# Chunked RWKV scan on one core: odd chunks cross the partition halves, and crossing and straight 64x64 products alternate

## What is computed

```python
def step(st, inp):
    r_t, w_t, k_t, v_t, a_t, b_t = inp
    sa = jnp.einsum('dbhij,dbhj->dbhi', st, a_t)
    st = st * w_t[..., None, :] + sa[..., None] * b_t[..., None, :] + v_t[..., None] * k_t[..., None, :]
    y = jnp.einsum('dbhij,dbhj->dbhi', st, r_t)
    return st, y
```

## Time and profile before

| | us |
|---|---|
| median of 3 runs | 3831.46 |
| lowest and highest | 3827.92 and 3834.9 |
| the profiled execution's own time | 3832.17 |
| its span in the trace | 3830.4 |
| the scan stage in the trace | 3019.6 to 3382.5 |

### The profile page before, as it was taken

How to read it: one execution, slowest core, us unless ns; L and a number is a source line. 1 busy time by engine, 2 the same in 40 slices (tenths; PEclk the granted TensorE clock), 3 DMA queues, 4 the chain that set the end, 5 groups by cost and what they waited for, 6 DMA issues and landing times.

```text
span 3830.4 us, 74936 instructions
## 1 busy us (share of the span) xinstructions
PE 3743.3 (98%) x30266; PEld 3432.7 (90%) x30266; DVE 2649.1 (69%) x3847; ACT 1868.0 (49%) x2450; POOL 0.2 (0%) x4
## 2 busy tenths in 40 slices
PE   8999999999999999999999999999999999999997
PEld 7999988999898888899988888888889899999896
DVE  6799977887755774667766656565766766666565
ACT  4444445444554544477455545454545433356653
POOL 0000000000000000000000000000000000000000
PEclk9999999999999999999999999999999999999999
DMA  5555544435554556544555555555564311134453
GB/s 194 176 182 185 176 146 163 163 118 195 186 176 171 195 185 220 190 154 169 191 182 187 187 187 189 187 187 190 176 227 156 123 58 47 47 117 154 163 195 134
DMA packets 99110, 634.90 MB, mean 166 GB/s; under 512 B 10864, under 2 KB 14320, under 8 KB 28720
## 3 DMA queue, kind: packets, MB, share of 16 engines
q1 hardware_dynamic: 98832, 631.00, 48.2%
HBM read 622.53 MB, written 8.42 MB: 165 GB/s over the span
## 4 chain that ended last, share of the span: by engine, by line
PE 88%; DVE 7%; ACT 2%; issue 1%; DMA 1%; SPq 0%; DVEq 0%; ACTq 0%
PE ps_gemm L355 33%; PE ps_gemm L344 18%; PE ps_gemm L357 17%; PE ps_gemm L341 6%; DVE ring_r L279 2%; PE ps_gemm L2107 2%; PE ps_aux L2107 2%; DVE arena L1384 1%; ACT w_hi L273 1%; PE ps_gemm L2066 1%; PE ps_aux L2066 1%; DVE arena L1681 1%; PE ps_aux L1794 1%; PE ps_gemm L2055 1%; PE ps_aux L1239 1%
## 5 line engine op out<-in xcount | busy, mean ns | idle before, releaser
L279 DVE TENSOR_TENSOR ring_r<-ring,w_hi 128x1024 fp32r<-128x1024 f32 (+3 forms) x1260 | 1411.7, 1126 | 876.5 <-ACT w_hi L273 862.0
L273 ACT ACTIVATE w_hi<-ring 128x1024 fp32r<-128x1024 f32 (+3 forms) x1260 | 1226.6, 979 | 1249.2 <-PE ps_gemm L355 703.8
L355 PE MATMUL ps_gemm<-arena_r,w_hi 128*128 128x512 f32 x5824 | 1471.4, 395 | 23.6 <-ACT w_hi L273 13.1
L355 PEld LDWEIGHTS ps_gemm<-arena_r,w_hi 128*128 128x128 f32 x5824 | 1052.2, 190 | 217.9 <-issue 23.1
L357 PEld LDWEIGHTS ps_gemm<-arena_r,ring_r 128*128 128x128 f32 x5824 | 795.6, 191 | 70.6 <-DVE ring_r L279 14.1
L357 PE MATMUL ps_gemm<-arena_r,ring_r 128*128 128x256 f32 x5824 | 814.9, 283 | 9.8 <-DVE ring_r L279 9.6
L344 PE MATMUL ps_gemm<-arena_r,w_hi 128*128 128x256 f32 (+2 forms) x4896 | 660.5, 284 | 7.8 <-ACT w_hi L273 6.8
L344 PEld LDWEIGHTS ps_gemm<-arena_r,w_hi 128*128 128x128 f32 (+2 forms) x4896 | 615.7, 190 | 13.3 <-ACT w_hi L273 7.5
L344 PE MATMUL ps_gemm<-arena_r,ring_r 128*128 128x256 f32 (+3 forms) x2448 | 364.7, 285 | 13.3 <-DVE ring_r L279 13.1
L344 PEld LDWEIGHTS ps_gemm<-arena_r,ring_r 128*128 128x128 f32 (+3 forms) x2448 | 321.2, 190 | 21.3 <-DVE ring_r L279 19.7
L1384 DVE SCALAR_TENSOR_TENSOR arena<-arena,vecs (+15 forms) x480 | 192.0, 462 | 0.0
(11 more groups left out here) (363 smaller groups left out, 2541.9 us busy)
## 6 DMA issues: line engine op xcount, KB each, us to landing
ring<-in_ff SPq DMA_DIRECT2D x128, 1024.0 KB, 4.9
ring<-in_w_out SPq DMA_DIRECT2D x48, 1024.0 KB, 4.9
ring<-in_gate SPq DMA_DIRECT2D x32, 1024.0 KB, 4.9
ring<-in_conv_a SPq DMA_DIRECT2D x16, 1024.0 KB, 5.3
ring<-in_conv_b SPq DMA_DIRECT2D x16, 1024.0 KB, 4.9
ring<-in_gla_v SPq DMA_DIRECT2D x16, 1024.0 KB, 4.9
ring<-in_conv_z SPq DMA_DIRECT2D x16, 1024.0 KB, 4.9
ring<-in_conv_out SPq DMA_DIRECT2D x16, 1024.0 KB, 4.9
```

The source lines that it names most:

```text
L273: nc.scalar.activation(w_hi[q % 2][:, 0:size], ring[slot][:, part], ACT.Copy).then_inc(hi_ready, 1)
L279: nc.vector.tensor_tensor(ring_lo[slot][:, part], ring[slot][:, part], w_hi[q % 2][:, 0:size].bitcast(F32), ALU.subtract).then_inc(lo_read ...
L355: mm = nc.tensor.matmul(halves, w, r_both[:, :, kk, :], start=q == 0 and k == 0, stop=False)
```

## The change

For odd chunks the two heads swap partition halves in every matrix that is indexed by token: `crossed` turns the output's half around for c = 1 and 3. Products from channel-indexed to token-indexed data, and back, then read one half of the partitions and write the other ("crossing"); for even chunks, and for all products of token by token, they stay in their half ("straight"). In tok, gram and the first half of w, `paired` issues a straight and a crossing product in turn; the results of even chunks go to one bank of XY and those of odd chunks to the other (`banked` tells the copies where they are). Where one bank (or the y bank) changes between straight and crossing writers, TensorE waits for its own earlier matmul: two new waits for `tiles_turned` per direction and iteration, five for `y_turned` per iteration. `TERMS` has a new order: the 22 terms are now spread as 4, 4, 2, 4, 1, 5, 2 over the seven places, before as 4, 4, 4, 4, 2, 2, 2. The number and shape of the matmuls is the same, on every engine.

```diff
-                q.XY = ps[:, 2:4, :].rearrange("p b n -> p (b n)") if d == 0 else ps[:, 0:2, :].rearrange("p b n -> p (b n)")
+                q.XY = ps[:, 2:4, :] if d == 0 else ps[:, 0:2, :]
...
+            def crossed(R, c):
+                return HALVES[1 - HALVES.index(R)] if c % 2 else R
+            def banked(bank2, blocks, n):
+                return bank2[:, :, 0:blocks * 2 * n].rearrange("p a (g n) -> p g a n", n=n)
+            def paired(straight, cross):
+                for pair in zip(straight, cross):
+                    for emit in pair:
+                        for R in HALVES:
+                            x = emit(R)
+                return x
...
                 if name == "tok":
-                    b = by(q.bk[:, 0, :])
-                    each(q.Z, AR[:, :, 0, :], b)
-                    v = by(channels(VD, it))
-                    for k, src in enumerate((AR[:, :, 0, :], by(q.bkp[:, 0, :]), by(q.bkp[:, 1, :]), v)[0:4 - d]):
-                        for c in range(NCH):
-                            for R in HALVES:
-                                x = mm(q.XY[R, (NCH * k + c) * CH:(NCH * k + c + 1) * CH], src[R, c, :], ident[R, R], start=True, stop=True)
+                    b, v = by(q.bk[:, 0, :]), by(channels(VD, it))
+                    sources = (AR[:, :, 0, :], by(q.bkp[:, 0, :]), by(q.bkp[:, 1, :]), v)[0:4 - d]
+                    def grams(c):
+                        return lambda R: mm(q.Z[crossed(R, c), c * CH:(c + 1) * CH], AR[R, c, 0, :], b[R, c, :], start=True, stop=True)
+                    def turned(k, c):
+                        at = (2 * k + c // 2) * CH
+                        return lambda R: mm(q.XY[crossed(R, c), c % 2, at:at + CH], sources[k][R, c, :], ident[R, R], start=True, stop=True)
+                    by_k = range(len(sources))
+                    paired([grams(0), grams(2)], [turned(0, 1), turned(0, 3)]).then_inc(tiles_turned, 1)
+                    paired([turned(k, c) for k in by_k for c in (0, 2)][:-2], [turned(k, c) for k in by_k[1:] for c in (1, 3)])
+                    pe.wait_ge(tiles_turned, 4 * it + d + 1)
+                    return paired([turned(by_k[-1], 0), turned(by_k[-1], 2)], [grams(1), grams(3)])
                 elif name == "gram":
-                    for k, bank in ((1, q.X), (0, q.Y)):
-                        for c in range(NCH):
-                            for R in HALVES:
-                                x = mm(bank[R, c * P:(c + 1) * P], q.bk[R, k, c * CH:(c + 1) * CH],
-                                       AR[R, c, :, :].rearrange("p k n -> p (k n)"), start=True, stop=True)
+                    def grams(k, c):
+                        at = (2 * k + c // 2) * P
+                        return lambda R: mm(q.XY[crossed(R, c), c % 2, at:at + P], q.bk[R, k, c * CH:(c + 1) * CH],
+                                            AR[R, c, :, :].rearrange("p k n -> p (k n)"), start=True, stop=True)
+                    return paired([grams(k, c) for k in (1, 0) for c in (0, 2)], [grams(k, c) for k in (1, 0) for c in (1, 3)])
...
                 elif name == "w":
-                    each(X0, q.tok[:, 0], q.TT)
-                    x = each(X1, q.TT, q.Z0)
+                    def weights(c):
+                        at = c // 2 * CH
+                        return lambda R: mm(q.XY[crossed(R, c), c % 2, at:at + CH], q.tok[R, 0, c, :], q.TT[R, c, :], start=True, stop=True)
+                    paired([weights(0), weights(2)], [weights(1), weights(3)]).then_inc(tiles_turned, 1)
+                    for c in (0, 2, 1, 3):
+                        if c == 1:
+                            pe.wait_ge(tiles_turned, 4 * it + d + 3)
+                        at = (2 + c // 2) * CH
+                        for R in HALVES:
+                            x = mm(q.XY[R, c % 2, at:at + CH], q.TT[R, c, :], q.Z0[R, c, :], start=True, stop=True)
                 elif name[0] == "u":
                     c = q.order[name[1]]
                     for R in HALVES:
-                        x = mm(q.Y[R, 0:CH], q.W1T[R, c, :], q.S[R, name[1], :], start=True, stop=True)
+                        x = mm(q.Y[crossed(R, c), 0:CH], q.W1T[R, c, :], q.S[R, name[1], :], start=True, stop=True)
                 elif name[0] == "s":
                     c = q.order[name[1]]
                     for R in HALVES:
-                        mm(q.Z[R, 0:CH], q.tok[R, 1, c, :], q.U[R, c, :], start=True, stop=False)
+                        mm(q.Z[crossed(R, c), 0:CH], q.tok[R, 1, c, :], q.U[R, c, :], start=True, stop=False)
                     for R in HALVES:
-                        x = mm(q.Z[R, 0:CH], q.tok[R, 2, c, :], VT[R, c, :], start=False, stop=True)
+                        x = mm(q.Z[crossed(R, c), 0:CH], q.tok[R, 2, c, :], VT[R, c, :], start=False, stop=True)
                 return x
-            TERMS = {("s", 0): (("v", 0), ("v", 1)), ("u", 1): (("v", 2), ("v", 3)), ("s", 1): (("u", 0), ("s", 1)), ("u", 2): (("u", 1), ("s", 2)),
-                     ("s", 2): (("u", 2),), ("u", 3): (("s", 3),), "end": (("u", 3),)}
-
-            def outputs(it, step):
+            TERMS = {("s", 0): (("v", 0, 0), ("v", 0, 1), ("v", 2, 0), ("v", 2, 1)),
+                     ("u", 1): (("v", 1, 0), ("v", 1, 1), ("v", 3, 0), ("v", 3, 1)),
+                     ("s", 1): (("u", 1, 0), ("u", 3, 1)),
+                     ("u", 2): (("u", 0, 0), ("u", 2, 1), ("s", 1, 0), ("s", 2, 1)),
+                     ("s", 2): (("u", 1, 1),),
+                     ("u", 3): (("u", 2, 0), ("s", 2, 0), ("s", 1, 1), ("s", 3, 0), ("s", 0, 1)),
+                     "end": (("u", 0, 1), ("u", 3, 0))}
+            TURNED = {("u", 1): 1, ("u", 2): 2, ("s", 2): 3, ("u", 3): 4}
+            def outputs(pe, it, step):
                 y = dirs[1].X
-                for kind, k in TERMS[step]:
-                    for d, q in enumerate(dirs):
-                        c = k if kind == "v" else q.order[k]
-                        left, right = {"v": (VT[:, c, :], q.M2[:, c, 1, :]), "u": (q.U[:, c, :], q.M1[:, c, 1, :]), "s": (q.S[:, k, :], q.AR[it % 2][:, c, 1, :])}[kind]
-                        for R in HALVES:
-                            x = nc.tensor.matmul(y[R, c * CH:(c + 1) * CH], left[R, :], right[R, :], start=step == ("s", 0) and k == 0 and d == 0,
-                                                 stop=step == "end" and d == 1, skip_group_check=True)
+                if step in TURNED:
+                    pe.wait_ge(y_turned, 5 * it + TURNED[step])
+                for kind, c, d in TERMS[step]:
+                    q = dirs[d]
+                    left, right = {"v": (VT[:, c, :], q.M2[:, c, 1, :]), "u": (q.U[:, c, :], q.M1[:, c, 1, :]),
+                                   "s": (q.S[:, q.order.index(c), :], q.AR[it % 2][:, c, 1, :])}[kind]
+                    if step == "end" and d == 0:
+                        x.then_inc(y_turned, 1)
+                        pe.wait_ge(y_turned, 5 * it + 5)
+                    for R in HALVES:
+                        x = nc.tensor.matmul(y[R if kind == "s" else crossed(R, c), c * CH:(c + 1) * CH], left[R, :], right[R, :],
+                                             start=step == ("s", 0) and c == 0 and d == 0, stop=step == "end" and d == 0, skip_group_check=True)
+                if step in (("s", 0), ("s", 1), ("u", 2), ("s", 2)):
+                    x.then_inc(y_turned, 1)
                 return x
...
-                    return cp(q.tok, q.XY[:, 0:256 * (4 - d)].rearrange("p (k c n) -> p k c n", k=4 - d, c=NCH))
+                    return cp(q.tok.rearrange("p k (g a) n -> p (k g) a n", a=2), banked(q.XY, 4 - d, CH))
...
-                    m = per_chunk(masks64[:, d, :, :].rearrange("p k t -> p (k t)"))
-                    for bank, M in ((q.X, q.M2), (q.Y, q.M1)):
-                        x = tt(M.rearrange("p c k t -> p c (k t)"), by(bank), m, ALU.mult)
+                    m = masks64[:, d, :, :].rearrange("p (a b k) t -> p a b (k t)", a=1, b=1).broadcast_to([P, 2, 2, P])
+                    for k, M in ((1, q.M2), (0, q.M1)):
+                        x = tt(M.rearrange("p (g a) k t -> p g a (k t)", a=2), banked(q.XY[:, :, k * 2 * P:(k + 1) * 2 * P], 1, P), m, ALU.mult)
```

More of the change, by code:

```diff
@@ L2029, in rwkv_scan @@
             VT = dirs[0].tok[:, 3]
-            prep_exp, chain, y_done, y_copied, started = stage_sems("exponentials", "dve_chain", "y_done", "y_copied", "states_zero")
+            prep_exp, chain, y_done, y_copied, started, y_turned, tiles_turned = stage_sems("exponentials", "dve_chain", "y_done", "y_copied", "states_zero", "y_tiles_turned", "tiles_turned")
             prepared = stage_sems("prepared0", "prepared1")
@@ L2097, in rwkv_scan, with pe_emit @@
             HALVES = (slice(0, CH), slice(CH, P))
+            def crossed(R, c):
[8 more added lines that the diff above has]
+                return x
             RATE = float(np.exp(-0.5))
-            def pe_emit(it, q, d, name):
+            def pe_emit(pe, it, q, d, name):
```

(8 more changed lines are left out.)

## The result

The changed kernel takes **3818.95 us** (median of 11 runs, 3815.12 to 3822.12); the kernel before took 3830.41 us in runs on the same chip (11 runs, 3827.0 to 3836.26). The ratio is 0.9969, with a 95% interval of 0.9962 to 0.9977: faster by 0.3%, 11.5 us. The forecast was 3817, 14.4 us from tok and gram. The profiled execution took 3819.21 us at a span of 3817.4.

The account below looks back on a forecast made before the run. TensorE is busy 98% of the span, but VectorE is late next and limits the gain. 3832.2 us less 7 x 2.06 = 14.4, plus 0.3, is 3818.1; the median lies 0.7 lower, say 3817; range 3809 to 3837.

Parts of the forecast that it names:

- tok and gram: Main term, scan stage: paired products let d2 start 2.06 us earlier in seven iterations, 14.4 us in all.
- I take the full overlap: In tok and gram all four corners run side by side, freeing 2.1 and 1.8 us per iteration, 3.9 in all.
- Shared loads: Rival, chance 0.12: corners in the same rows load in turn, 64 columns gain nothing, only gram halves; 3824 us.
- Exposed loads: Rival, chance 0.12: each paired matmul waits about 55 ns for a load, 26 us in all; 3861 us, tok 6 us.
- 60% of the full overlap is enough; what is late next is thus VectorE: In tok and gram TensorE need free only 2.4 of its 3.9 us per iteration, as VectorE then limits.
- VectorE's wait before gram's masks: VectorE's 1.33 us idle before its gram masks would be gone in iterations 2 to 8.
- they come 1.33 us earlier and no more: Bound on gram's masks: VectorE cannot begin them before its last tok mask ends, at 3076.60.
- The slack before d2: d2, started 0.78 us after VectorE was done, behind projection pieces, would start some 0.05 us after it.
- w: 16 of 32 matmuls paired, against two waits of 0.1 us: -0.27 to +0.2 us per iteration, taken as 0.
- The waits for y: Four of five nearly free; the fifth, 0.3 us per iteration, hidden in seven iterations by late VectorE, 0.3 us left.
- TERMS and the walk: New order of terms in the chain over chunks: taken as 0, with 0.1 us per iteration to either side.
- The first iteration: The spill holds VectorE there whatever TensorE does, so nothing is gained; VectorE's wait still about 5 us.

Follow-up runs that it names:

- no_cross: Changed kernel with odd chunks' heads back on their own halves, so no product crosses; waits, order, TERMS and two-bank reads kept: 3834.01 us, 1.0009 of the kernel before.
- seq_all: Changed kernel with tok, gram and w issuing all straight products of a block first, then all crossing ones: 3823.59 us, 0.9979 of the kernel before.

## Why the prediction was right, and where it was not

- **The time and its sign: right.** 3818.95 for 3817, in the range, faster by 0.31% (0.23 to 0.38). That it came within 2 us is in part luck: the main term, tok and gram, gave half of what I took, and others that I had put at nothing made up for it (last point).
- **The rates: right.** "I take the full overlap": 27 ns and 15 ns per record for 55 and 29. Shared loads would have left tok's records at 29 ns; they fell too. Exposed loads would have taken tok to 6 us; it is 3.61. The rule of the Trainium skill, "TensorE: Matmul & The Clock Gate", Part 3, by which a weight load overlaps a running matmul only where the row group differs, does not hold here for halves of columns in the same rows. Each corner keeps the 58 ns per matmul, loads included, that it had with its neighbour idle, and TensorE loads for 2.37 us of the 2.65 in which it multiplies in tok. The 25 ns between two starts that the same page of the Trainium skill gives (Part 1) is no floor over several corners: here it is 15.
- **"60% of the full overlap is enough; what is late next is thus VectorE": the step that failed.** Full overlap came, and yet tok and gram gave 0.59 and 0.58 us in the second iteration, 1.17 of 3.9, not the 2.4 that I wanted, because TensorE paused for instructions, 1.4 us per iteration on average (9.6 / 7). VectorE's wait before gram's masks, a term of 1.33 us, was not gone: 8.5 us for 9.3 in seven iterations, 0.1 each. The masks still came 0.58 us earlier. Most of that is a wait that the prediction did not have, as the second iteration, from which it was read, has none of it: in the later ones VectorE waits for tok before tok's own masks. Iterations 2 to 8, before (L2207) and after (L2252):

```profile
DVE arena L2207 <- PE ps_aux L2118: 2.3, 4, 1.4
DVE arena L2207 <- PE ps_gemm L2118: 1.1, 1, 1.1
```

```profile
DVE arena L2252 <- PE ps_aux L2132: 0.5, 1, 0.5
DVE arena L2252 <- PE ps_gemm L2132: 0.3, 1, 0.3
```

That is 3.4 us, now 0.8, or 0.4 per iteration. So "they come 1.33 us earlier and no more" was a bound of the second iteration alone. The slack before d2, a term of 0.73 (0.78 - 0.05), gave 0.50: in six iterations d2 starts 3.1 us after the first mask, 0.62 earlier than before, and in the one shown 3.97, later than before, as it waits for the delayed pieces. Together 1.08 for 2.06. There was a warning in the trace of before, in gram of the first iteration, and "issue" with 1% of the chain in the earlier trace rows:

```profile
3027.12 0.76 PE L2123 MATMUL ps_gemm<-arena 64*64 64x128 f32 x10 [1.95 <-issue]
```

I treated the supply of instructions as free.
- **w: mis-sized to the good side.** I took 0 between ends of -0.27 and +0.2. From w's first record to the projection piece 2.02 us became 1.71 (and below), -0.31, just past the low end: the second kind of products starts at 3061.30, while the first still runs, so the waits that were to eat up the gain do not show.

```profile
3061.02 0.46 PE L2177 MATMUL ps_gemm<-arena 64*64 64x64 f32 x16
3061.30 0.66 PE L2184 MATMUL ps_gemm<-arena 64*64 64x64 f32 x14
...
3062.73 0.74 PE L2055 MATMUL ps_gemm<-arena_r,ring_r 128*128 128x256 f32 x4
```

- **The waits for y: right.** The fifth is `L2220 <- L2220`, 1.6 us in 8 times, 0.2 each for 0.3. The other four leave no row. That it hides behind a late VectorE was not separately tested.
- **TERMS and the walk:** 0 with 0.1 to 0.3 to the good: -0.14 per iteration from s0 to the end of U. In no_cross, which has the new TERMS, the same stretch is 5.22 for 5.21: the gain is of the crossing, in s, u or the terms.
- **The first iteration: right that VectorE gains nothing there;** its wait for the spill is 7.7 us for 5.5. It hid the longest pause as well, 4.2 us.
- **Why the sum still came close.** Per iteration 0.98 us of gain was missing (1.08 for 2.06) and 0.43 was not counted (w and the walk): -0.55, times 7 is 3.9 us. Outside the seven iterations the kernel gained 0.9 (11.5 between the medians, less 10.6 in the traces) where I had a loss of 0.3, and the kernel before was 1.05 us faster in these runs than in those that I had: 3.9 - 1.2 - 1.05 = 1.6 us above 3817.4. Of these only the 3.9 is read from the same two traces; the other two are no larger than the differences between single runs.

## What to carry to other kernels

Two products on the same partitions but in different column halves of the array run fully side by side here, with their outputs in separate banks (no run tried one bank), so an idle corner is worth filling by swapping halves. But count instructions as well as time: in this kernel a stretch of small float32 matmuls that wanted more than one of them per 58 ns stood still, once or twice per iteration, for its own instruction packets, and then its time depended on what was issued long before it. Where a small edit moves the time by 10 us and the trace shows "issue" in new places, try the same edit with another number of idle instructions before you believe in its mechanism.

## What the runs showed of the hardware

- TensorE's instructions come in 16 KB packets of about 256. All 15 pauses of the changed kernel's stage end 2.2 to 2.9 us after a packet starts (3069.12 to 3071.48, 3072.74 to 3075.28), the next packet starts 1.0 to 1.7 us after that end, and so two pauses in a row, one packet apart, are 3.5 to 4.3 us apart. What sets these times was not taken apart.
- 64 and 128 added instructions that compute nothing, once, put the same kernel at 0.9997 and 0.9957 of the kernel before.
- Straight and crossing blocks issued one after the other still overlap (44 ns per gram record, for 55 on two corners and 27 in turns), so TensorE does not wait with a corner's work until the other corners' is done. In seq_all's single records of that gram, the first crossing pair starts at 3115.16 and the last straight one, issued before it, at 3115.47. "TensorE works strictly through its list", as the text ahead of the prediction has it, thus holds for its waits, not for the starts of products on different corners.
- The clock did not enter: the three windows of tok, gram and the pieces were granted 1.00 before and after, the upper of TensorE's two levels, 2.4 GHz.
